# The filler products of the first experts' stage, left out in its last four steps

## The chip, the cores and the metric

The kernel runs on one core of one Trainium2 chip. The metric is the time of one execution on the device, in microseconds (us), as the median of several runs.

## The reference, cut to what matters

Two transformer blocks run one after the other over 512 tokens of width 1024. Each ends with a mixture of experts. The first block's is this one:

```python
for g in range(N_GROUPS):                       # 4 groups of 8 experts
    sl = slice(g * EXPERTS_PER_GROUP, (g + 1) * EXPERTS_PER_GROUP)
    a = jnp.einsum('nd,edf->nef', hf, w_g[sl])  # gate, 1024 -> 256
    u = jnp.einsum('nd,edf->nef', hf, w_u[sl])  # up,   1024 -> 256
    hid = jax.nn.silu(a) * u * gates[:, sl, None].astype(hf.dtype)
    out = out + jnp.einsum('nef,efd->nd', hid, w_d[sl]).astype(jnp.float32)
```

`gates` is zero but for two of the 32 experts of a token, so an expert has to be computed only for the rows of the tokens that chose it. All is in float32.

## The kernel before, in words

The kernel is one long program of stages. The stage of this case is `paired_experts_stage`, run by `first_experts` for the first block's 32 experts. It takes the experts in 16 pairs; each expert of a pair has 64 of the 128 places for rows. The loop over the steps i from -4 to 16 is a software pipeline, written out for each engine.

On TensorE, step i does, in this order: the two transposes of the hidden rows of pair i-1 (L1669); the gate and up products of pair i (L1681, 32 instructions; they wait for the pair's weights, semaphores `gu_in`); the transposes of the gathered rows of pair i+1 (L1694); the list of rows of pair i+3 (L1703); the down products of pair i-1 (L1717, 16 instructions; they wait for `d_in`, the down weights, and for the copy of the transposed hidden rows, `ht_copied`); and last, if there is a pair i, `keep_clock(K, pe, b_ht, 4)` (L1721, whose products stand at L1175). Those four products multiply two constant tiles into the bank `b_ht`. The next transposes overwrite the bank, and nothing reads the products in between. They carry no wait and no signal. A product of `keep_clock` is float32 and is recorded as two instructions, so four of them are a row of x8. They are called fillers below.

ScalarE and VectorE apply silu and the gate (L1777, L1732), copy the turned rows (L1783, L1739) and hidden rows (L1771), and copy the down product out of its banks (L1789, L1761). GpSimd's queue gathers the rows of a pair from memory (L1804) and adds a pair's output rows to the accumulator in memory (`scatter_add`, L2328). The scatter of pair i-1 waits for both copies of its down product and for the landing of the scatter before it.

SyncE's queue loads the weights. An expert's gate, up and down matrices are 1 MB each. The order is written out by hand in the last function below: for pair p it waits for the gate/up product of pair p-3, issues the four gate/up loads of pair p (L1607), waits for the down product of pair p-3, and issues the two down loads of pair p-1 (L1611). So the gate/up loads of pair 15, the last ones, stand behind the wait for the down product of pair 11, which TensorE does in step 12. The down loads of pair 14 wait for the down product of pair 12 (step 13), and those of pair 15 for that of pair 13 (step 14). After the loads the queue waits for all 16 scatters, and only then loads the first weights of the next stage (L227, `load_jobs`). An overflow stage stands between, which has nothing to do on this data, and then the second block starts on TensorE with six products of `keep_clock` (L2568).

Of the kernel before, what the change touches and what calls it, by code (L numbers as in the profile page):

```python
# [1171 lines left out]
def keep_clock(K, pe, bank, n):  # L1172

    for _ in range(n):
        pe.matmul(bank[:, :], K.ident[:, :], K.causal[:, :], start=True, stop=True)  # L1175
# [452 lines left out]
def paired_experts_stage(K, m, weights, next_vectors):  # L1628
# [28 lines left out]
    has = lambda i, d: 0 <= i + d < N  # L1657

    with nc.Block(no_gpsimd_drain=True) as block:
        @block.tensor  # L1660
        def _(pe):
            for i in steps:
                if has(i, -1):
                    b = (i - 1) % 2
                    pe.wait_ge(hid_ready, i)
                    if i >= 2:
                        pe.wait_ge(ht_copied, i - 1)
                    for j in range(FH):
                        mm = pe.transpose(b_ht[:, P * j:P * j + P], hid[:, b, j::FH], K.ident[:, :])  # L1669
                    mm.then_inc(ht_mm, 1)  # L1670
                if has(i, 0):
                    b, places = i % 2, weights.PLACES[i % 3]
                    for copied in xt_copied:
                        pe.wait_ge(copied, i + 1)
                    for q in places:
                        pe.wait_ge(gu_in[q], 32 * (i // 3 + 1))
                    if i >= 2:
                        pe.wait_ge(hid_ready, i - 1)
                    for c in range(KC):
                        for n, part in enumerate(rows):  # L1680
                            mm = pe.matmul(b_au[b][part, :], xt[:, b, P * c + HALF * n:P * c + HALF * n + HALF],  # L1681
                                           gu[places[n]][:, :, c, :], start=c == 0, stop=c == KC - 1)
                    mm.then_inc(au_mm, 1)
                if has(i, 1):
                    b = (i + 1) % 2
                    if i < 0:
                        keep_clock(K, pe, K.bank[6], 5)
                    pe.wait_ge(gathered[b], 16 * ((i + 1) // 2 + 1))
                    if i >= 0:
                        for copied in xt_copied:  # L1690
                            pe.wait_ge(copied, i + 1)
                    for half in range(2):
                        for k in range(4):
                            mm = pe.transpose(b_xt[half][:, P * k:P * k + P], xg[:, b, 4 * half + k::KC], K.ident[:, :])  # L1694
                        mm.then_inc(xt_mm, 1)
                if has(i, 3):
                    b = (i + 3) % 2
                    pe.wait_ge(listed, i + 4)
                    if i >= -2:
                        pe.wait_ge(idx_ready, 2 * i + 6)  # L1700
                    for n, part in enumerate(rows):
                        for t in range(T):
                            mm = pe.matmul(b_list[part, 0:5], onehot[:, b, t, part], m.parts[:, t, weights.pairs[i + 3][n], 0:5],  # L1703
                                           start=t == 0, stop=t == T - 1)
                    mm.then_inc(list_mm, 1)
                if has(i, -1):
                    b, places = (i - 1) % 2, weights.DOWN_PLACES[(i - 1) % 2]
                    pe.wait_ge(ht_copied, i)
                    for q in places:
                        pe.wait_ge(d_in[q], 16 * ((i - 1) // 2 + 1))  # L1710
                    if i >= 2:
                        pe.wait_ge(y_dve, i - 1)
                        pe.wait_ge(y_act, i - 1)
                    for half in range(2):
                        for j in range(FH):
                            for n, part in enumerate(rows):
                                mm = pe.matmul(b_y[half][part, :], hidt[:, b, P * j + HALF * n:P * j + HALF * n + HALF],  # L1717
                                               dn[places[n]][:, j, 512 * half:512 * half + 512], start=j == 0, stop=j == FH - 1)
                    mm.then_inc(y_mm, 1)
                    if has(i, 0):  # L1720
                        keep_clock(K, pe, b_ht, 4)  # L1721

        @block.vector
# [1550 lines left out]
```

## Time and profile before

| | |
|---|---|
| median of 3 runs | 1876.27 us (1872.62 to 1878.36) |
| the profiled execution's own time | 1880.13 us |
| its span in the profile | 1878.4 us |
| its mean granted TensorE clock | 0.933 |
| TensorE busy with products | 1646.6 us (88% of the span) |
| VectorE / ScalarE / GpSimd busy | 647.4 / 438.7 / 478.6 us |
| first experts' stage, gate/up products | from 444.1 us to 693.3 us of the span |

The profile comes from one execution. Its span is what the engines' records cover; the execution's own time is measured from outside and is 1.7 us longer. TensorE's busy time is no measure of its rate, since products overlap and their ends are modelled. Where one product's end matters, the start of the next instruction is used.

### The profile page before, as it was taken

Reading aid. Unit: us, or ns where it says so; the run is one execution under the profiler, and the core shown is the slowest. Engines: PE = TensorE matmul, PEld = TensorE weight load, DVE = VectorE, ACT = ScalarE, POOL = GpSimd, SP = SyncE. Lnnn points to the kernel's source line nnn. Section 1 sums busy time; section 2 is a strip of 40 time slices with the busy share of each in tenths; the row PEclk is TensorE's granted clock in tenths of the full one; section 3 lists DMA queues with packets and bytes.
Section 4 is the critical chain, followed back from the end, with each engine's and each line's share of the span. In section 5 each row is a group of like instructions: output and inputs, shape, how many; then the busy total and the mean of one; then the engine's idle time right before and its main releaser. Section 6 shows DMA issues by size and latency. Waiting matters only on the chain. (4 is left out here: it accounts for less than half of the span.)

```text
span 1878.4 us, 21926 instructions
## 1 busy us (share of the span) xinstructions
PE 1646.6 (88%) x7996; PEld 906.2 (48%) x7996; DVE 647.4 (34%) x1630; ACT 438.7 (23%) x945; POOL 478.6 (25%) x385
## 2 busy tenths in 40 slices
PE   6989999898999895999999969989998788887882
PEld 3334445774333333678678857644433333332330
DVE  1785615432111115662363334532222221221212
ACT  3412215421111014563453222211110000000001
POOL 3997916001111103770110000012221111111110
PEclk9799999988999997999999979989998888998996
DMA  5353320457999964512202246658999999999974
GB/s 201 135 171 132 134 90 5 169 213 276 398 407 404 399 240 162 180 46 95 91 1 90 90 142 239 246 221 309 389 390 395 376 369 370 376 369 365 368 288 163
DMA packets 110807, 446.23 MB, mean 238 GB/s; under 512 B 20356, under 2 KB 24852, under 8 KB 73320
## 3 DMA queue, kind: packets, MB, share of 16 engines
q1 hardware_dynamic: 94824, 411.13, 56.6%
q0 software_dynamic: 15840, 33.60, 7.1%
q8 instruction: 68, 1.11, 0.2%
q14 instruction: 43, 0.35, 0.1%
q10 hardware_dynamic: 32, 0.04, 0.0%
HBM read 427.33 MB, written 44.10 MB: 251 GB/s over the span
## 5 line engine op out<-in xcount | busy, mean ns | idle before, releaser
L2007 PE MATMUL bank<-big,heads 128*32 128x512 f32 (+2 forms) x1040 | 261.2, 661 | 51.7 <-DMA big<-in_w_exp_up_dram 35.1
L2007 PEld LDWEIGHTS bank<-big,heads 128*32 128x32 f32 (+2 forms) x1040 | 83.5, 139 | 175.4 <-issue 173.9
L2328 POOL DMA_INDIRECT acc_scratch<-heads,small x55 | 87.2, 1585 | 249.2 <-DVE heads L2092 158.0
L460 PE MATMUL bank<-big,h_cols 128*128 128x512 f32 x320 | 143.6, 603 | 0.3 <-ACT heads L610 0.3
L2058 DVE SCALAR_TENSOR_TENSOR heads<-heads,small,bank 128x256 f32<-128x256 f32 x39 | 18.7, 480 | 352.4 <-ACT heads L2110 352.4
L2132 POOL DMA_INDIRECT heads<-h_scratch,small x39 | 40.4, 1035 | 340.8 <-DVE small L2075 339.6
L1175 PE MATMUL bank<-causal,ident 128*128 128x512 f32 x174 | 91.3, 674 | 15.1 <-PEq L178 15.1
L2007 PE MATMUL bank<-junk_and_spare,heads 128*32 128x512 f32 (+2 forms) x272 | 84.2, 647 | 20.0 <-DMA big<-in_w_exp_up_dram 20.0
L2110 ACT ACTIVATE heads<-bank 128x256 f32<-128x256 f32 x39 | 15.0, 383 | 359.3 <-PE bank L2007 359.3
L818 POOL TENSOR_SCALAR junk_and_spare<-junk_and_spare,cond 128x512 f32<-128x512 f32 x56 | 97.2, 1736 | 5.5
L460 PEld LDWEIGHTS bank<-big,h_cols 128*128 128x128 f32 x320 | 60.0, 192 | 76.9 <-issue 76.4
L1114 PE MATMUL bank<-big_parts,x_res_parts 128*128 128x512 f32 x224 | 88.3, 394 | 0.0
L1681 PE MATMUL bank<-big,heads 128*64 128x512 f32 x352 | 82.2, 621 | 6.1 <-DMA big<-in_w_exp_up_dram 5.3
L2092 DVE TENSOR_TENSOR heads<-bank,gain 128x512 f32<-128x512 f32 x78 | 50.2, 686 | 103.0 <-PE bank L2042 103.0
L2007 PE MATMUL bank<-h_cols,heads 128*128 128x512 f32 (+2 forms) x160 | 75.6, 628 | 0.0
L821 POOL TENSOR_TENSOR h_rows<-h_rows,junk_and_spare 128x512 f32<-128x512 f32 x56 | 74.1, 1324 | 4.7
L2123 POOL MEMSET heads<- 128x2048 f32 x1 | 1.8, 1805 | 285.4 <-POOLq L1195 285.4
L1732 DVE SCALAR_TENSOR_TENSOR heads<-heads,small,bank 128x256 f32<-128x256 f32 x16 | 7.7, 480 | 176.2 <-ACT heads L1777 176.2
L1175 PEld LDWEIGHTS bank<-causal,ident 128*128 128x128 f32 x174 | 35.2, 212 | 65.8 <-issue 65.8
L1113 PE MATMUL bank<-big_parts,x_res_parts 128*128 128x512 f32 x160 | 63.4, 396 | 2.0 <-DVE big_parts L1098 2.0
L933 PE MATMUL bank<-heads,big 128*128 128x64 f32 x480 | 64.0, 266 | 0.6 <-DVE h_rows L997 0.4
L1115 PE MATMUL bank<-big_parts,h_cols_parts 128*128 128x512 f32 x160 | 63.0, 394 | 0.0
(475 smaller groups left out, 3224.3 us busy)
## 6 DMA issues: line engine op xcount, KB each, us to landing
big<-in_w_exp_gate_dram SPq DMA_DIRECT2D x65, 1024.0 KB, 16.5
big<-in_w_exp_up_dram SPq DMA_DIRECT2D x65, 1024.0 KB, 27.1
x_res<-in_w_exp_down_dram SPq DMA_DIRECT2D x38, 1024.0 KB, 26.7
h_rows<-in_w_exp_down_dram SPq DMA_DIRECT2D x28, 1024.0 KB, 31.6
big<-in_w_in_dram SPq DMA_DIRECT2D x13, 2048.0 KB, 9.0
junk_and_spare<-in_w_mod_dram SPq DMA_DIRECT2D x24, 1024.0 KB, 5.4
big<-in_w_exp_down_dram SPq DMA_DIRECT2D x19, 1024.0 KB, 18.0
junk_and_spare<-in_w_exp_gate_dram SPq DMA_DIRECT2D x16, 1024.0 KB, 18.8
```

The source lines that it names most:

```text
L460: mm = pe.matmul(out, lhsT, rhs, start=c == 0, stop=c == len(lhs_rhs) - 1)
L818: ins = pool.tensor_scalar(acc if first else w[:, c, :], w[:, c, :], cond, None, ALU.mult)
L821: ins = pool.tensor_tensor(acc, acc, w[:, c, :], ALU.add)
L933: mm = pe.matmul(K.bank[5 + u % 2][:, 0:64], turn[:, u % 3, P * k:P * k + P], K.v[:, k, 64 * h:64 * h + 64], start=k == 0, stop=k == t)
L1113: pe.matmul(banks[t][:, :], a_high, high, start=c == 0, stop=False)
L1114: pe.matmul(banks[t][:, :], a_high, low, start=False, stop=False)
L1115: mm = pe.matmul(banks[t][:, :], a_low, high, start=False, stop=c == n - 1)
L1175: pe.matmul(bank[:, :], K.ident[:, :], K.causal[:, :], start=True, stop=True)
L1681: mm = pe.matmul(b_au[b][part, :], xt[:, b, P * c + HALF * n:P * c + HALF * n + HALF], gu[places[n]][:, :, c, :], start=c == 0, stop=c == ...
L2007: mm = pe.matmul(b_au[b][tile, :], xt[:, b, P * c + tile.start:P * c + tile.stop], gu[places[n][0]][:, :, c, :], start=c == 0, stop=c == K ...
L2092: dve.tensor_tensor(ys[:, b, cols], b_y[half][:, :], K.gain[:, cols], ALU.mult).then_inc(y_taken, 1)
L2328: return pool.indirect_dma_start(out=acc, out_offset=bass.IndirectOffsetOnAxis(at, 0), in_=rows, in_offset=None, bounds_check=acc.shape[0] ...
```

## The change

The fillers' condition asks for a pair i+4 in place of a pair i. There are pairs 0 to 15, so the fillers of steps 12, 13, 14 and 15 are left out, and those of steps 1 to 11 stay. Nothing else is changed.

```diff
                                 mm = pe.matmul(b_y[half][part, :], hidt[:, b, P * j + HALF * n:P * j + HALF * n + HALF],
                                                dn[places[n]][:, j, 512 * half:512 * half + 512], start=j == 0, stop=j == FH - 1)
                     mm.then_inc(y_mm, 1)
-                    if has(i, 0):
+                    if has(i, 4):
                         keep_clock(K, pe, b_ht, 4)
```

with, in this function, `has = lambda i, d: 0 <= i + d < N` and N = 16.

## Rows read from the trace of the kernel before

**Rows 1.** The page: its first line, and the chain that ended last, by line.
```profile
span 1878.4 us, 21926 instructions
...
PE bank L2007 8%; SPq L1559 7%; DMA big<-in_w_exp_up_dram 4%; DMA h_cols<-in_w_exp_up_dram 3%; PE bank L2042 3%; SPq L1563 3%; DMA junk_and_spare<-in_w_exp_up_dram 2%; PE bank L2020 1%; DMA acc_scratch<-heads,small 1%; SPq L1553 1%; DMA big<-acc_scratch 0%; DMA heads<-h_scratch,small 0%; DVE h_rows L3225 0%; PE bank L1995 0%; PE bank L2029 0%
```

**Rows 2.** Timeline of PE: start us, us, engine, line, form; in brackets the idle time before.
```profile
597.84 7.09 PE L1681 MATMUL bank<-big,heads 128*64 128x512 f32 x32 [1.03 <-DMA big<-in_w_exp_up_dram]
...
645.43 3.70 PE L1175 MATMUL bank<-causal,ident 128*128 128x512 f32 x8
...
653.62 8.78 PE L1681 MATMUL bank<-big,heads 128*64 128x512 f32 x32 [4.26 <-DMA big<-in_w_exp_up_dram]
...
667.01 3.70 PE L1175 MATMUL bank<-causal,ident 128*128 128x512 f32 x8
670.55 0.39 PE L1669 MATMUL bank<-ident,heads 128*128 128x128 f32 x2
670.87 0.64 PE L1681 MATMUL bank<-h_cols,heads 128*64 128x512 f32 x1
...
682.56 3.70 PE L1175 MATMUL bank<-causal,ident 128*128 128x512 f32 x8
...
686.42 7.09 PE L1681 MATMUL bank<-big,heads 128*64 128x512 f32 x32
693.33 0.59 PE L1717 MATMUL bank<-big,heads 128*64 128x512 f32 x1
...
696.87 3.70 PE L1175 MATMUL bank<-causal,ident 128*128 128x512 f32 x8
...
701.27 3.65 PE L1717 MATMUL bank<-x_res,heads 128*64 128x512 f32 x16 [0.47 <-ACT heads L1771]
```

**Rows 3.** Timeline of SP's queue: when four of the loads were issued.
```profile
620.18 0.43 SPq L1607 DMA_DIRECT2D big<-in_w_exp_up_dram  x1
...
639.32 2.14 SPq L1607 DMA_DIRECT2D junk_and_spare<-in_w_exp_up_dram  x1
...
658.17 2.10 SPq L1607 DMA_DIRECT2D big<-in_w_exp_up_dram  x1
...
667.49 0.43 SPq L1611 DMA_DIRECT2D h_rows<-in_w_exp_down_dram  x1
```

**Rows 4.** DMA issues at 620, 639, 658, 667 and 683 us; last, us to landing.
```profile
big<-in_w_exp_up_dram SPq DMA_DIRECT2D x1, 1024.0 KB, 33.2
...
junk_and_spare<-in_w_exp_up_dram SPq DMA_DIRECT2D x1, 1024.0 KB, 30.4
...
big<-in_w_exp_up_dram SPq DMA_DIRECT2D x1, 1024.0 KB, 27.9
...
h_rows<-in_w_exp_down_dram SPq DMA_DIRECT2D x1, 1024.0 KB, 25.6
...
x_res<-in_w_exp_down_dram SPq DMA_DIRECT2D x2, 1024.0 KB, 13.9
```

**Rows 5.** Windows: stretch, length, busy by engine, granted PE clock, DMA share, GB/s.
```profile
613.59:616.00 2.41, 0.00 (x0) 0.03 (x1) 0.00 (x0) 0.38 (x1) 0.00 (x0) 1.00 1.04 425
616.00:624.72 8.72, 8.71 (x32) 3.13 (x33) 0.00 (x0) 0.00 (x0) 0.00 (x0) 0.80 1.02 389
...
653.60:662.34 8.74, 8.72 (x33) 3.18 (x33) 0.00 (x0) 0.00 (x0) 0.00 (x0) 0.80 1.00 406
```

**Rows 6.** Timeline at the stage's end: the last two scatters and what follows them.
```profile
696.99 0.69 DVE L1761 COPY heads<-bank 128x512 f32<-128x512 f32 x1 [2.54 <-PE bank L1717]
...
698.54 1.56 POOL L2328 DMA_INDIRECT acc_scratch<-heads,small  x1 [12.75 <-DVE heads L1761]
...
706.53 1.56 POOL L2328 DMA_INDIRECT acc_scratch<-heads,small  x1 [6.43 <-DVE heads L1761]
...
712.53 1.27 SPq L227 DMA_DIRECT2D big<-in_w_in_dram  x2
```

**Rows 7.** Line L2328 alone, from 698 to 699 us: issue to landing.
```profile
DMA to landing us min/median/max: 6.2/6.2/6.2
```

## The prediction

> **What bounds the kernel now.** I read the page first. Its chain that ended last names only lines of the second block's experts, and its shares add up to about a third of the span [rows 1]. So it does not reach back to the stage that is changed, and that stage has to be read by itself. What it is worth is told by its far end: SyncE issues the first weights of the next stage at 712.53 us, which is the moment at which the last scatter lands, 6.0 us after its issue at 706.53 [rows 6]. All later work stands behind these loads, and nothing of it was begun before. A microsecond by which the last scatter comes earlier or later is therefore one microsecond of the kernel, and what doesn't reach that scatter is worth nothing.
>
> The timeline of TensorE comes next. In the last steps its work looks unbroken: gate/up of pair 14 from 670.87, fillers from 682.56, gate/up of pair 15 from 686.42, down of pair 14 from 693.33, fillers from 696.87, down of pair 15 from 701.27 [rows 2]. The one visible stall is the 4.26 us before the gate/up of pair 13 at 653.62, put down to a weight load [rows 2]. A reader who stops here takes three of the four sets of fillers to be on the path.
>
> The landings say otherwise, and they are the centre of the case. Issue time plus time to landing gives: pair 13's last gate/up weights at 620.18 + 33.2 = 653.4, pair 14's at 639.32 + 30.4 = 669.7, pair 15's at 658.17 + 27.9 = 686.1, and pair 14's last down weights at 667.49 + 25.6 = 693.1 [rows 3, 4]. The first is checked by the stall: the product starts at 653.62, 0.24 us after its weights have landed. The others stand 1.1, 0.35 and 0.24 us ahead of the products that need them. So the fillers end just as the weights arrive. TensorE and the DMA queues are level, and the queues come in a hair earlier.
>
> **The change part by part.** It removes four times four products, 32 instructions and their 32 weight loads. One set takes 670.55 - 667.01 = 3.54 us [rows 2], and four take 14.2 us of TensorE. It adds no instruction, wait or semaphore, and moves no order. Whether the loads come earlier: the last gate/up loads wait for the down product of pair 11, which ends before the first removed set at 645.43 [rows 2]. They are issued and land as before. Pair 14's down loads wait for the down product of pair 12, done at 667.01, before the second removed set can tell. Only pair 15's down loads, behind the down product of pair 13, can move.
>
> *Step 12 (fillers at 645.43).* The gate/up of pair 13 waits for 653.4 in any case. Worth 0; the gap ahead of it grows from 4.26 to 7.8 us.
>
> *Step 13 (667.01).* Fillers and two transposes took 3.86 us up to 670.87 [rows 2]. Without the fillers TensorE is free at 667.4, waits for the landing at 669.7 and starts at 669.95: 0.9 us gained, and a gap of 2.6 us that was not there.
>
> *Step 14 (682.56).* The gate/up of pair 15 can start at 686.1 + 0.24 = 686.3 and not before, against 686.42. So it gains 0.1 us, whatever step 13 gave, and a second new gap opens, of 2.6 to 4.2 us.
>
> *Step 15 (696.87).* The down product of pair 15 can come up to 3.5 us earlier. Its scatter however also waits for the scatter of pair 14, issued at 698.54, which lands after 6.2 us, at 704.7 [rows 6, 7]. POOL took 698.54 - (696.99 + 0.69) = 0.86 us from its releaser to its issue [rows 6]. Hence the last scatter can't be issued before 704.7 + 0.86 = 705.6, against 706.53. Fillers that are worth 3.5 us on TensorE bring 0.9 us, and the scatter of pair 14 is late next. Pair 15's down loads took 13.9 us from an issue just after 682.56 [rows 2, 4], so they are there by about 697, and the product needs them at about 698.
>
> Sum without an effect of the clock: -0.1 (step 14) and -0.9 (step 15), together -1.0 us.
>
> *The price of the gaps.* Before the gate/up of pair 10 TensorE sat idle for 1.03 us, and the 32 products took 7.0 us (7.09 with the modelled end) [rows 2]. After 2.41 us of idleness, for pair 11, they took 8.72 us at a mean granted clock of 0.80; after 4.3 us, for pair 13, 8.74 us at 0.80 [rows 5]. So part of the product ran at 1.2 in place of 2.4 GHz, and one such start costs 8.7 - 7.0 = 1.7 us. The new gaps of 2.6 us and more are nearest to the two that cost something, and I take 1.7 us for each. The Trainium skill has a rule against this change, in "TensorE: Matmul & The Clock Gate", section "Why this matters for your kernels": TensorE should not be left idle between bursts of matmuls, or the next burst starts at half clock. [...]
>
> Where the 1.7 us go: pair 13 paid them already. On pair 14 they are absorbed: it ends at 669.95 + 8.7 = 678.7 in place of 677.9, the down product of pair 13 follows at 683.4, and TensorE is ready for pair 15 at 683.8, still 2.3 us ahead of the weights. On pair 15 they aren't absorbed: gate/up 686.3 to 695.0, down of pair 14 to 698.5 in place of 696.87, its scatter issued at 700.2 and landed at 706.4, the last scatter issued at 707.2 in place of 706.53. So +0.7 us.
>
> **Forecast.** -1.0 + 1.7 = +0.7 us. Against the profiled execution's own 1880.13 us that is 1880.8, and against the median of the runs 1876.27 + 0.7 = 1877.0 us. The profiled execution lies 3.9 us above that median, more than any term here; the sum is a difference and carries over. Bounds: below, -1.0; above, one more cold start than I count on the path (the last down product, or a longer cold stretch for pair 13 after its gap of 7.8 us), 0.7 + 1.7 = +2.4.
>
> **Rivals.** (a) *Warm at pair 15.* The clock comes back in time, or doesn't fall, since TensorE works at full clock up to a gap of about 2.5 us. For it: the clock stayed whole after 1.03 us. Against: 2.41 us were enough once. Time 1876.27 - 1.0 = 1875.3 us.
>
> (b) *The fillers were on the path.* The landings come from one execution; if the last weights of pairs 14 and 15 usually come several microseconds sooner, steps 13 and 14 give their full 3.54 us each and step 15 its 0.9: -8.0 us, 1868.3 us. For it: TensorE's unbroken timeline. Against: the four landings, which stand right behind one another, and the stall of pair 13, which shows the queues behind TensorE.
>
> (c) *The clock stays down.* After 7.8 us of idleness the gate/up of pair 13 runs all through at 1.2 GHz, 14.0 in place of 8.7 us, which delays the down loads of pair 14, and so does that of pair 15, 14 in place of 7 us. Price 5.3 + 7.0 - 1.0 = +11.3 us, 1887.6 us. It decides once more than about 6.6 us beyond the sum are lost, which is nearly the whole of one gate/up product at half clock. Against: after 4.3 us of idleness the clock was back within the product, at a mean of 0.80.
>
> That the edit doesn't do what it says is no rival: the condition holds for i up to 11, and only four steps lose their fillers.
>
> **How the numbers follow.** A measurement of this kernel can tell about 0.3%, 5.6 us, from no change. Forecast 0.52, (a) 0.34, (b) 0.08, (c) 0.06. The first two lie within 0.3%, (b) is faster and (c) slower. The range takes in the first two with their bounds and the spread of the runs: 1872.6 - 1.0, some 1871.7, to 1878.4 + 2.4, some 1880.8.
>
> **What would show it right or wrong.** In the changed kernel's trace: L1175 with 32 instructions fewer; gate/up of pairs 14 and 15 with a wait for a weight load of some 2.5 us each, starting near 669.9 and 686.3; their length, 8.7 against 7.0 us, with the granted clock, decides between the forecast and (a); the last scatter issued 0.86 us behind the landing of the one before. Starts of pair 15's gate/up at 680 us or earlier would make (b) right and the forecast wrong; a gate/up product of 14 us would make it (c).

## The result, and the profile after

The changed kernel takes 1885.7 us (median of 20 runs, 1875.96 to 1894.94), the kernel before 1877.57 us (median of 20, 1871.56 to 1887.81). The ratio is 1.0045, with a 95% interval of 1.0033 to 1.0058: slower by some 8.4 us by that ratio. The forecast was 1877.0 us, no change, in a range up to 1880.8; the result lies outside of it.

The page of the changed kernel has the same picture as before, with the same lines in the chain [rows 1]; only TensorE's counts differ, by the 32 instructions. The profiled execution took 1887.68 us.

```profile
span 1886.0 us, 21862 instructions
...
PE 1639.7 (87%) x7964; PEld 903.3 (48%) x7964; DVE 643.3 (34%) x1630; ACT 438.6 (23%) x945; POOL 478.1 (25%) x385
```

I look at the changed stage first. TensorE's timeline in the last steps, answering to [rows 2]:

```profile
650.86 9.12 PE L1681 MATMUL bank<-big,heads 128*64 128x512 f32 x32 [7.52 <-DMA big<-in_w_exp_up_dram]
...
667.26 0.61 PE L1681 MATMUL bank<-h_cols,heads 128*64 128x512 f32 x1 [2.16 <-DMA junk_and_spare<-in_w_exp_up_dram]
...
683.52 9.85 PE L1681 MATMUL bank<-big,heads 128*64 128x512 f32 x32 [4.07 <-DMA big<-in_w_exp_up_dram]
...
693.19 0.59 PE L1717 MATMUL bank<-big,heads 128*64 128x512 f32 x1
...
697.79 3.65 PE L1717 MATMUL bank<-x_res,heads 128*64 128x512 f32 x16 [0.55 <-ACT heads L1771]
```

All three gate/up products now wait for a weight load, as the prediction's steps 12 to 14 said. The loads answer to [rows 3, 4]. Here are the issues of pair 14's and pair 15's last gate/up weights, on SyncE's queue:

```profile
636.56 2.14 SPq L1607 DMA_DIRECT2D junk_and_spare<-in_w_exp_up_dram  x1
...
655.41 2.11 SPq L1607 DMA_DIRECT2D big<-in_w_exp_up_dram  x1
```

And here are their times to landing, from the DMA view at 636 and 655 us:

```profile
junk_and_spare<-in_w_exp_up_dram SPq DMA_DIRECT2D x1, 1024.0 KB, 30.5
...
big<-in_w_exp_up_dram SPq DMA_DIRECT2D x1, 1024.0 KB, 27.9
```

They land at 667.1 and 683.3, and the products start 0.2 us later. To landing they took 30.4 and 27.9 us before, so the loads themselves are no slower without the fillers. What the gaps cost, the windows of the changed kernel tell (columns as in [rows 5]):

```profile
650.86:659.91 9.05, 9.05 (x32) 2.93 (x32) 0.00 (x0) 0.00 (x0) 0.00 (x0) 0.77 1.01 409
667.26:674.28 7.02, 7.02 (x33) 2.62 (x33) 0.00 (x0) 0.00 (x0) 0.61 (x1) 1.00 0.92 347
683.52:693.19 9.67, 9.67 (x32) 3.27 (x34) 0.00 (x0) 0.00 (x0) 0.00 (x0) 0.71 0.55 159
```

Pair 14's product stayed at full clock after a gap of 2.16 us; pair 15's took 9.67 us, 2.7 us more than at full clock. The end of the stage answers to [rows 6]:

```profile
698.40 1.56 POOL L2328 DMA_INDIRECT acc_scratch<-heads,small  x1 [16.22 <-DVE heads L1761]
705.27 1.56 POOL L2328 DMA_INDIRECT acc_scratch<-heads,small  x1 [5.30 <-DMA acc_scratch<-heads,small]
...
711.19 1.27 SPq L227 DMA_DIRECT2D big<-in_w_in_dram  x2
```

The last scatter now waits for the one before it and not for VectorE's copy, as forecast. From the end of pair 11's down product to the first load of the next stage, the changed kernel takes 711.19 - 642.84 = 68.4 us, before 712.53 - 645.43 = 67.1 us. The stage accounts for 1.3 us in this pair of traces. At its end the changed kernel is even 1.3 us ahead of the other trace (711.19 against 712.53), and it still ends 7.6 us behind (1886.0 against 1878.4). **The loss lies behind the stage, in code that the change doesn't touch.**

To find it I compared the starts of the same instruction in both traces. The largest step is between ScalarE's copy L1278 at 1176.89 and its copy L2116 at 1263.07 (before), the passage from the second block's output stage through its router and shared expert to its first experts. It takes 86.2 us before and 92.8 us in the changed kernel. Three rows of the kernel before, from the timelines of VectorE and TensorE there:

```profile
1201.15 2.29 DVE L3172 TENSOR_TENSOR heads<-heads,gain 128x2048 f32<-128x2048 f32 x1 [13.24 <-DMA gain<-mod_scratch]
1203.50 0.43 DVE L3068 TENSOR_TENSOR keep_mask<-keep_mask,small 128x256 f32<-128x256 f32 x1
...
1217.93 1.23 PE L3131 MATMUL bank<-ident,heads 128*128 128x128 f32 x8 [1.20 <-DVE heads L3164]
```

The same three of the changed kernel:

```profile
1200.09 2.29 DVE L3172 TENSOR_TENSOR heads<-heads,gain 128x2048 f32<-128x2048 f32 x1 [14.68 <-DMA gain<-mod_scratch]
1202.30 0.42 DVE L3068 TENSOR_TENSOR keep_mask<-keep_mask,small 128x256 f32<-128x256 f32 x1
...
1216.70 1.23 PE L3131 MATMUL bank<-ident,heads 128*128 128x128 f32 x8 [2.45 <-DVE heads L3164]
```

VectorE multiplies the shared expert's down weights by a row (`gain`, the "gate row" below), whose load is the last of a burst on SyncE's queue: four weight loads of 1 MB, a store, then the row. Behind that multiply, in order, stands the router's chain (L3068 to L3164), on which TensorE waits at L3131. Before, the multiply ended at 1203.44, within 0.1 us of the moment at which the router's input came from ScalarE (L3062 ended at 1203.38), and L3068 started at 1203.50: nothing was lost, and nothing was to spare. In the changed kernel that input was there at 1200.9, and VectorE turned to it at 1202.30. So TensorE stands idle for 2.45 us and not 1.20, and then this happens (windows of the changed kernel):

```profile
1214.25:1216.70 2.45, 0.00 (x0) 0.00 (x0) 2.33 (x7) 0.39 (x1) 0.00 (x0) 1.00 0.56 157
1216.70:1228.40 11.70, 11.70 (x43) 8.65 (x44) 4.96 (x25) 1.68 (x3) 0.00 (x0) 0.56 0.13 57
```

Before, in the same stretch:

```profile
1217.90:1228.20 10.30, 10.27 (x52) 6.64 (x53) 6.72 (x31) 2.28 (x4) 0.00 (x0) 1.00 0.28 113
```

The mean granted clock is 0.56 in these 11.7 us, so most of them run at 1.2 GHz, while the other engines wait for TensorE; before it is 1.00. That the row is late is seen in line L3167, issue to landing. Before:

```profile
DMA to landing us min/median/max: 15.2/15.2/15.2
```

In the changed kernel:

```profile
DMA to landing us min/median/max: 17.1/17.1/17.1
```

What differs nearby is a packet of 16 KB on an instruction queue, q8. I take it for the queue with which the sequencer fetches TensorE's program, because its packets move when TensorE's program alone is edited (from 1182.68 us before to 1176.86 in `p16_before` and 1192.05 in `p48_before`, both below). The DMA view of before has it in the stretch from 1182 to 1184 us, at the burst's start; that of the changed kernel in the stretch from 1187 to 1189 us, in its middle:

```profile
q8 instruction: 1, 0.02, 3.8%
```
```profile
q8 instruction: 1, 0.02, 3.1%
```

On the common time axis this is 7 us later. The change took 64 instructions (32 products and their weight loads) out of TensorE's program, so every later piece of it lies elsewhere in those fetches. The Trainium skill describes them in "Runtime: NRT & Kernel Launch", section "Instruction fetch mechanics": blocks of 16 KiB, 256 instructions, fetched one after the other, and a branch out of the window waits for its page. It also says that straight-line fetching is hidden. In this stretch the trace agrees: from 1174 to 1230 us the one wait between TensorE's products is that at L3131, for VectorE. What a fetch pushes aside is another matter, and the experiments ask for it.

**The theories.** Position ("layout" in the first expectations): the loss comes from where TensorE's later program lies, through the late row. Stage: it arises in the changed stage, by cold starts (products that begin at 1.2 GHz behind a gap), more than one trace shows. Chance: two sets of runs differ for no cause. Clock behind the stage: the later stages start from another state of the clock.

### The profile page after: what moved, and what is told of

The parts are those of the page before. It is cut to its first block and busy times, and to the rows that moved or that the text cites. A ratio compares the mean times of both kernels' runs of the same rounds, so it can differ in the third digit from the quotient of the medians.

```text
span 1886.0 us, 21862 instructions
## 1 busy us (share of the span) xinstructions
PE 1639.7 (87%) x7964; PEld 903.3 (48%) x7964; DVE 643.3 (34%) x1630; ACT 438.6 (23%) x945; POOL 478.1 (25%) x385
## 5 line engine op out<-in xcount | busy, mean ns | idle before, releaser
L2328 POOL DMA_INDIRECT acc_scratch<-heads,small x55 | 87.2, 1586 | 253.4 <-DVE heads L2092 154.5
L1175 PE MATMUL bank<-causal,ident 128*128 128x512 f32 x142 | 74.9, 677 | 17.3 <-PEq L178 17.3
L2042 PE MATMUL bank<-x_res,heads 128*32 128x512 f32 (+2 forms) x272 | 62.0, 596 | 1.1 <-DVE heads L2092 1.1
```

Of the source, the lines that this page charges most:

```text
L2042: mm = pe.matmul(b_y[half][tile, :], hidt[:, b, P * j + tile.start:P * j + tile.stop], dn[places[n][0]][:, j, 512 * half:512 * half + 512] ...
L2328: return pool.indirect_dma_start(out=acc, out_offset=bass.IndirectOffsetOnAxis(at, 0), in_=rows, in_offset=None, bounds_check=acc.shape[0] ...
```

## The experiments

**The two kernels again.** `c0_control` is the kernel before, unchanged.

> The kernel before, unchanged, against itself. Theory stage (the loss arises between the first removed fillers and the last scatter): ratio 1.000. Theory layout (with 32 products fewer, everything behind the stage lies elsewhere in TensorE's program, and that costs): 1.000. Theory chance (two sets of runs differ by 0.4% without a cause): a ratio away from 1 by 0.003 or more is possible here, and that would show it.

Measured: 1878.3 against 1878.43 us, ratio 0.9997 (0.9984 to 1.0011).

`c1_after_again` is the changed kernel, unchanged.

> The changed kernel again. Theories stage and layout: ratio near 1.0045 as measured before. Theory chance: near 1.000. In the trace, from the start of the transposes that follow the down product of pair 11 to the last scatter's landing, the stage theory wants several us more than the 67.1 us from 645.43 to 712.53 of before; the first changed trace had 68.4.

Measured: 1887.76 us, ratio 1.0055 (1.0038 to 1.0072). Chance falls. In its trace the part from the end of pair 11's down product to the first load took 707.94 - 644.97 = 63.0 us, the shortest of all traces here: against the stage theory.

**The same program length.** `c2_tiny_at_end` is the changed kernel with as many instructions put back as were taken out, where TensorE has nothing to do:

```diff
                     if has(i, 4):
                         keep_clock(K, pe, b_ht, 4)
+                    if i == N:
+                        for _ in range(16):
+                            pe.matmul(b_ht[:, 0:8], K.ident[:, :], K.causal[:, 0:8], start=True, stop=True)
```

> The changed kernel with 16 products of 8 columns at the very end of the stage, where TensorE has nothing to do: as many instructions as before, so every later stage lies where it lay before. Theory layout: the loss is gone, ratio within 0.001 of 1.000. Theory stage: the loss stays, ratio 1.004 or more. Theory clock behind the stage (the later stages lose because TensorE comes to them at another state of its clock): 1.004 too, with the time lost after the last scatter.

Measured: 1878.47 us, ratio 0.9994 (0.9981 to 1.0006). The fillers are gone, and so is the loss.

**One step alone.** `d15_only` has `has(i, 0) and i != 15` as the condition.

> Only the fillers of step 15 left out, those of steps 12 to 14 kept. The gate/up products of pairs 13 to 15 keep their cover, so no new cold start ahead of them. Theory stage with cold starts: ratio 0.9995, the last scatter 0.9 us earlier. Theory clock behind the stage: the stretch of idleness before the next stage grows by 3.5 us, and if that is what costs, the ratio is 1.003 or more. Theory layout: 8 of the 32 instructions are gone, ratio between 1.000 and 1.0045.

Measured: 1877.86 us, ratio 0.9997 (0.9988 to 1.0006). TensorE's longer idleness before the next stage, 16.83 us in its trace against 15.13, costs nothing.

**Early, not at the end.** `c3_tiny_early` puts the 16 small products ahead of a wait for gathered rows instead:

```diff
                     if i < 0:
                         keep_clock(K, pe, K.bank[6], 5)
+                    if i == -1:
+                        for _ in range(16):
+                            pe.matmul(b_ht[0:8, 0:8], K.ident[:, 0:8], K.causal[:, 0:8], start=True, stop=True)
```

> The changed kernel with 16 small products early in the stage (ahead of a wait for gathered rows), so that TensorE's program behind the stage lies where it lay before, and nothing is added at the stage's end. Theory program position: ratio 0.998 to 1.001, as with the small products at the end. Theory of the products at the end (they kept the clock or changed the hand-over to the next stage): the loss is back, 1.0045. In the trace, the 16 KB fetch of TensorE's program near 1182 us lies just before the weight loads of that place, and the load of the gate row lands some 15 us after its issue, not 17.

Measured: 1876.07 us, ratio 1.0002 (0.9987 to 1.0017); the row landed 14.6 us after its issue. Not the products at the stage's end, but the position behind them is what heals.

**The loss without the change.** `p48_before` keeps every filler and only moves what follows:

```diff
                     if has(i, 0):
                         keep_clock(K, pe, b_ht, 4)
+                    if i == N:
+                        for _ in range(48):
+                            pe.matmul(b_ht[0:8, 0:8], K.ident[:, 0:8], K.causal[:, 0:8], start=True, stop=True)
```

> The kernel before, with all its fillers, and 48 small products at the stage's end: TensorE's program behind the stage lies 192 instructions later, which in fetches of 16 KB (256 instructions) is the same place as 64 earlier, that of the changed kernel. Theory program position: slower, ratio 1.003 to 1.006, the gate row lands 17 us after its issue. Theory stage, or missing fillers: 1.000, or what 48 small products cost in an idle stretch, nothing.

Measured: 1887.8 us, ratio 1.0059 (1.0039 to 1.0079). The small products took 2.55 us in an idle stretch, and the next stage started 7.53 us after its first load, as before. This kernel shows the changed kernel's loss with none of its change. The 48 small products are 192 instructions more (a product in f32 is issued as two, each with its weight load); the change has 64 fewer. The two are 256 instructions apart, one packet of 16 KB by the Trainium skill's figure in the section named above, so what follows lies in the same place of a packet. The same rows of it, in its own line numbers (3 higher), and line L3170's time to landing:

```profile
1205.47 2.29 DVE L3175 TENSOR_TENSOR heads<-heads,gain 128x2048 f32<-128x2048 f32 x1 [15.08 <-DMA gain<-mod_scratch]
1207.68 0.42 DVE L3071 TENSOR_TENSOR keep_mask<-keep_mask,small 128x256 f32<-128x256 f32 x1
```
```profile
1222.12 1.33 PE L3134 MATMUL bank<-ident,heads 128*128 128x128 f32 x8 [2.90 <-DVE heads L3167]
```
```profile
DMA to landing us min/median/max: 17.6/17.6/17.6
```

**Taking the late row away.** `g_after` and `g_before` move the gate row's load ahead of the two experts' gate/up loads, in the changed kernel and in before. The store of the last tile (L1379) goes ahead of those loads with it:

```diff
                         shared.load_down(sp)
-                    next_weights(1)
+                    if not shared:
+                        next_weights(1)
                 sp.wait_ge(added, T + t + 1)
...
                     shared.load_gate(sp)
+                    next_weights(1)
                 sp.wait_ge(normed, t + 1)
```

> The changed kernel, with the load of the gate row on the SyncE queue of the second block's output stage moved ahead of four weight loads of 1 MB. If the loss comes through the late landing of that row (VectorE's multiply by it then stands in the router's way, TensorE waits, its clock falls), the ratio to before is 0.998 to 1.001. If the late row is only a bystander, 1.0045 stays.

> The kernel before with the same move of the gate row's load. If the row is late only in the changed kernel: 0.999 to 1.001. If it is late in some executions of before too, a gain, 0.997 to 0.999.

Measured: `g_after` 1879.11 us, ratio 1.0017 (1.0001 to 1.0033); `g_before` 1877.74 us, 1.0006 (0.9988 to 1.0024). More than half of the loss goes with this move, not all of it. In both traces TensorE's wait at L3131 is back to 1.20 us, at a granted clock of 1.00 from there on. In before nothing was late, and nothing is gained.

`p48_g` does the same to `p48_before`, which has all the fillers:

> The kernel before with all its fillers, 48 small products at the stage's end, and the gate row's load ahead of the weights. Where 48 small products alone cost 0.59%, the theory of the late gate row wants most of it back: 1.000 to 1.002. In the trace the stretch from the second block's output stage to its first experts (from 1176.9 to 1263.0 us in before, 86.2 us long, and 91 to 93 us in the shifted kernels) is back at 84 to 86 us. If the row is a bystander, 1.005 to 1.006 stays.

Measured: 1878.21 us, ratio 1.0013 (1.0002 to 1.0023), against 1.0059 without the move. The multiply is done early, and TensorE's wait is back to 1.19 us:

```profile
1185.75 2.29 DVE L3177 TENSOR_TENSOR heads<-heads,gain 128x2048 f32<-128x2048 f32 x1 [2.30 <-DMA gain<-mod_scratch]
```
```profile
1213.48 1.22 PE L3136 MATMUL bank<-ident,heads 128*128 128x128 f32 x8 [1.19 <-DVE heads L3169]
```

**Other positions.** `p16_before` and `p32_before` are `p48_before` with 16 and 32 small products.

> The kernel before with 16 small products at the stage's end: what lies behind the stage is 64 instructions later, so its program fetches come earlier than in before. Theory program position: the gate row's load, which follows a fetch by 3 us in before and precedes it by 4 us in the changed kernel, is now well clear of it; it lands in 14.5 to 15.2 us and the ratio is 0.998 to 1.001. If any move of the program costs, 1.003 or more.

> The same with 32 small products, 128 instructions later. Theory program position: the fetch near the gate row's load is another 9 to 17 us away and no other stands in its place; ratio 0.998 to 1.001, unless a fetch falls on another tight place, which the segments of the trace would show. With this, four of the positions that a fetch can have (0, 64, 128, 192 instructions) have been run.

Measured: 1881.15 us, ratio 1.0025 (1.0012 to 1.0037), and 1879.79 us, 1.0025 (1.0012 to 1.0038). Both expectations missed. The row was in time (14.9 and 15.9 us), but the hand-over to the next stage was not: SyncE issues the first load at 709.52, and TensorE starts at 722.43, 12.9 us later, where before needed 720.06 - 712.53 = 7.5 us. The row of `p16_before`:

```profile
722.43 7.44 PE L1175 MATMUL bank<-causal,ident 128*128 128x512 f32 x12 [19.34 <-PEq L178]
```

In `p32_before` the same stretch took 12.9 us as well. In both traces the engines start the next stage together, behind a barrier (L178): in `p16_before` SyncE's next load is issued at 722.38. What holds them up is in the traces too. It is a branch of TensorE's sequencer, that around the overflow stage (L2196; L2199 with the lines added). Before, and in `p16_before`:

```profile
L2196 PEldq COMPARE_BRANCH  x1: 378/378/378, 715.5 to 715.5; - x1
```
```profile
L2199 PEldq COMPARE_BRANCH  x1: 5845/5845/5845, 712.5 to 712.5; - x1
```

The branch took 5.8 to 5.9 us in the three traces with a hand-over of 12.9 us (`p16_before`, `p32_before`, `g_after`) and 0.4 to 0.5 us in the eleven with 7.5 us, and that is the whole difference of 5.4 us. The three also have two fetches of TensorE's program, 3.3 us apart, in this stretch. That agrees with what the same section of the Trainium skill says of a branch out of the window; why it should be so in these three alone, no trace shows. The position theory needs a second place; it isn't one row alone. That these 5.4 us are the loss of the runs is argued: the profiled execution of `p32_before` had the long branch too and still was among the shortest of its runs (1876.06 us), with a first stretch of 706.3 us.

**What the fetch does to the burst.** The landings of the burst's loads, one by one, say more than that of the row. The second expert load of the changed kernel, issued at 1180.55, landed after 10.2 us at 1190.7, and the one before it at 1180.08 + 7.0 = 1187.1: 3.6 us apart. In `p16_before`, with no fetch near, the same two landed at 1184.20 + 8.8 = 1193.0 and 1183.73 + 6.8 = 1190.5, 2.5 us apart. In that order:

```profile
big<-in_w_exp_gate_dram SPq DMA_DIRECT2D x1, 1024.0 KB, 7.0
...
big<-in_w_exp_up_dram SPq DMA_DIRECT2D x1, 1024.0 KB, 10.2
```
```profile
big<-in_w_exp_gate_dram SPq DMA_DIRECT2D x1, 1024.0 KB, 6.8
...
big<-in_w_exp_up_dram SPq DMA_DIRECT2D x1, 1024.0 KB, 8.8
```

The fetch at 1187.26 falls between the two landings. In all five traces with a fetch there (the change, `c1_after_again`, `p48_before`, `p48_g`, `g_after`) the load in flight landed 3.6 to 4.0 us behind the one before it, in the nine others 2.5 us. The packet itself took 3.1% of 16 engines over 2 us, so one engine for some 1.0 us, which is an estimate from the line above and near the 1.1 us in question.

**Both cures.** `g_c2` is `g_after` with 16 small products at the stage's end.

> The changed kernel with both cures: 16 small products at the stage's end and the gate row's load ahead of the weights. The position is that of before, and the row was not late there: 0.998 to 1.001, the same as either cure alone at its best. Below 0.998 it would be the version to keep.

Measured: 1876.91 us, ratio 1.0010 (0.9997 to 1.0022). No version here beats the kernel before by more than the measurement can tell.

**By stretch.** The starts of the same instruction in each trace, in us: to the first load of the second block (L227); from it to ScalarE's L1278 of the second tile; from there to its second L2116; from there to the end.

| trace | to the load | to L1278 | to L2116 | to the end | row to landing |
|---|---|---|---|---|---|
| before | 712.5 | 464.4 | 86.2 | 615.3 | 15.2 |
| c0_control | 705.6 | 462.1 | 85.8 | 616.0 | 14.7 |
| g_before | 708.0 | 463.2 | 85.8 | 616.5 | 6.4 |
| c2_tiny_at_end | 710.4 | 465.2 | 86.5 | 615.3 | 15.1 |
| c3_tiny_early | 707.9 | 463.2 | 83.8 | 615.5 | 14.6 |
| g_c2 | 709.8 | 463.0 | 83.8 | 615.0 | 6.4 |
| the change | 711.2 | 463.2 | 92.8 | 618.7 | 17.1 |
| c1_after_again | 707.9 | 467.0 | 90.8 | 614.9 | 17.3 |
| p48_before | 712.1 | 467.3 | 93.2 | 616.1 | 17.6 |
| p48_g | 708.9 | 463.5 | 85.6 | 617.5 | 6.1 |
| g_after | 710.9 | 472.7 | 84.0 | 618.0 | 6.5 |
| p16_before | 709.5 | 468.5 | 86.6 | 616.3 | 14.9 |
| p32_before | 706.3 | 465.8 | 86.0 | 616.2 | 15.9 |
| d15_only | 710.9 | 462.5 | 90.3 | 615.8 | 15.7 |

The three traces in the changed kernel's position with the row behind the weights (the change, `c1_after_again`, `p48_before`) need a mean of 92.3 us for the third stretch; the four with their fetches in the old position and the old order (before, `c0_control`, `c2_tiny_at_end`, `c3_tiny_early`) 85.6. That is 6.7 us of the loss. For the second stretch the means are 465.8 and 463.7, another 2 us, within the spread of single traces; so are the 3.4 us that the first trace of the change has more in the last stretch, as `c1_after_again` has 614.9 there. `d15_only`'s trace shows the late row too, though its runs aren't slower: the profiled execution was the slowest of its runs. It has 16 of the 64 instructions less. Its fetch lies 3.4 us ahead of the row's issue, as in before, so a fetch in the middle of the burst is not the only way to a late row. The row was issued 9.6 us behind L1278 and not 8.9, and landed at 25.3 and not 24.2; with nothing to spare that was enough for a wait of 2.17 us at L3131.

## Why the prediction was wrong, and where it was right

*What bounds the stage: right.* The landings decide. All four last weights land as long after their issue as before, and none of steps 12 to 14 pays in time.

*Step 12, worth 0, and step 13, 0.9 us and a gap of 2.6 us: right.* The gaps were 7.5 and 2.2 us in the first trace; in `c1_after_again` they were 3.7 and 4.1 us.

*Step 14, no gain: right. Step 15, limited by the scatter before it: right.* The trace names that scatter as the last releaser.

*The price of the gaps: right in kind, loose in size.* Over the traces a start behind a gap cost between nothing and 2.8 us, not always 1.7: pair 14's product was at full clock behind 2.16 us in one trace, and took 9.80 us behind 4.14 us in `c1_after_again`. The length of the gap alone doesn't decide, and rival (a)'s limit of about 2.5 us isn't there: `g_before` has a product of 7.02 us at full clock behind 2.80 us, and `g_c2` one of 8.71 us at 0.80 behind 2.18 us. The rule that the prediction quotes from the Trainium skill ("TensorE: Matmul & The Clock Gate", section "Why this matters for your kernels") is one for long gaps: behind the changed kernel's gaps of 7.5 and 4.1 us the trace agrees with it (mean clocks of 0.77 and 0.71 over the products), and the one of 2.2 us, at full clock, isn't covered by it.

*The sum of the stage: right in size, its sign not resolved.* The forecast was +0.7 us; the traces differ among themselves by more. The time from the end of pair 11's down product to the next stage's first load was, with the fillers, 67.1, 65.6, 66.3, 66.8, 64.4, 67.5 and 66.3 us (before, `c0_control`, `g_before`, `p16_before`, `p32_before`, `p48_before`, `p48_g`), and without them 68.4, 63.0, 66.0, 64.5, 67.0 and 65.4 us (the change, `c1_after_again`, `c2_tiny_at_end`, `c3_tiny_early`, `g_after`, `g_c2`). The means are 66.3 and 65.7. By runs, `c2_tiny_at_end` and `c3_tiny_early` leave the fillers out at 0.9994 and 1.0002. So the four sets of products, 14.2 us of TensorE, are worth nothing within 0.2% either way.

*The step that failed* is in the first part: "A microsecond by which the last scatter comes earlier or later is therefore one microsecond of the kernel, and what doesn't reach that scatter is worth nothing." That treats everything behind the stage as a rigid block. It is rigid as to data: nothing crosses the boundary but the accumulator. It isn't as to TensorE's program, of which 64 instructions fewer go ahead of the rest. The prediction put that at nothing; the runs gave some 8.4 us, of which 6.7 lie in the one stretch with the late row. Rival (c) had the sign, and its 1887.6 us comes near the measured 1885.7 by luck, as its cause is absent: no gate/up product behind these gaps took 14 us. Its chance of 0.06 was too small for a direction of which I had priced one mechanism only. A slip besides: the lower end of the range, 1872.6 - 1.0, is some 1871.6 and not 1871.7, which changes nothing.

*What is shown and what is argued.* Shown: the loss follows the position of TensorE's later program and not the fillers (gone with 16 small products in either place; there with 48 and all fillers). Shown: moving the gate row's load ahead takes most of it away, 0.0045 and 0.0055 down to 0.0017, and 0.0059 down to 0.0013. Shown in all fourteen traces: a fetch in the middle of the burst goes with 1.1 to 1.5 us of delay of the load in flight, and a hand-over of 12.9 us with a branch of 5.8 us on TensorE. Argued: that this first delay is the start of the row's. In the three traces where it is late by 2 us, the fetch lies 4.3 to 4.6 us behind the row's issue, in the traces of the old position with the old order 2.9 to 3.2 us ahead of it; but the fourth load of the burst adds about another 1.1 us (4.4 us behind the third in the changed kernel, 3.3 in `p16_before`), for which I have no cause. Open: the rest of 0.0013 to 0.0017, and what decides whether the branch is long. `g_after`'s profiled execution, the longest of its runs with 1887.28 us, had the long one, and the two traces of the changed kernel, with the same program of TensorE, the short one. Its runs reach from 1875.3 to 1887.3 us, so the long branch in some of them may be the rest; no trace shows the others.

## What to carry to other kernels

When a change adds or drops instructions of an engine in the middle of a long straight program, all that follows on that engine lies elsewhere in its program fetches; here that was worth between 0 and 0.6%, more than the edit itself. So compare at equal length: put as many cheap instructions back at an idle place and measure that too, before you credit or blame the edit. And look at the far side of the program for a place that has only a fraction of a microsecond to spare, such as a load on which an engine's whole queue waits, put behind four larger ones. A stretch that looks unchanged in length can have a margin of 0.1 us in it, as the multiply here.

## What the runs showed of the hardware that I had not expected

- The instruction queue q8 carried 68 packets of 16 KB before and 67 in the changed kernel, and the position of TensorE's program in them matters more here than the products that were dropped: four positions, 64 instructions apart, gave ratios of 1.000, 1.0025, 1.0025 and 1.0045 to 1.0059.
- A hand-over between two stages took 7.5 or 12.9 us from the same program of TensorE (the changed kernel and `g_after`), through one branch of its sequencer: 0.47 or 5.75 us.
- A wait of TensorE that grew by 1.25 us, from 1.20 to 2.45, led to 4.9 us in what followed it (L3143's third row of products starts at 1226.41 before and at 1230.06 in the changed kernel, whose start at L3131 was 1.23 us earlier), as the clock fell behind it.
